# Second mixer of a two-block transformer kernel: the two value units of the differential heads side by side as a pair of 512 columns, the other heads' query and key units behind them, and the forget gate's logarithm later

## What is computed

```python
proj = h @ w_in                      # 1024 -> 3*512 + 3*512 + 8
dq, dk, dv = ...                     # differential: 4 heads, each with two query/key maps of 64, values of 128
fq, fk, fv = ...                     # forget gate: 8 heads of 64
f_logit = proj[..., o:o + FOX_HEADS].astype(jnp.float32) + b_f
cum = jnp.cumsum(jax.nn.log_sigmoid(f_logit), axis=1)
...
sd = jnp.einsum('bqhd,bkhd->bhqk', qd, dk) * (DIFF_HEAD_DIM ** -0.5) + bias
pd = jax.nn.softmax(jnp.where(causal, sd, NEG_2), axis=-1)
ad = pd[:, :, 0] - lam * pd[:, :, 1]
od = jnp.einsum('bhqk,bkhe->bqhe', ad, dv)
...
sf = jnp.einsum('bqhd,bkhd->bhqk', qf, fk) * (FOX_HEAD_DIM ** -0.5) + cq - cum_k
pf = jax.nn.softmax(jnp.where(causal, sf, NEG_2), axis=-1)
of = jnp.einsum('bhqk,bkhd->bqhd', pf, fv)
```

## Time and profile before

| | us |
|---|---|
| median of 3 runs | 845.45 (845.39 to 845.58) |
| the profiled execution | 845.1 |
| its span | 843.3 |
| TensorE busy | 829.5 (98%) |
| VectorE busy | 597.8 (71%) |
| ScalarE busy | 473.9 (56%) |
| mean granted clock of TensorE | 0.999 of full |

### The profile page before, as it was taken

One profiled execution on the slowest core, in us unless ns is written; L12 is line 12 of the kernel. 1 busy time (PEld: TensorE's weight loads), 2 busy tenths in 40 slices (PEclk: granted clock), 3 DMA queues, 4 the chain that ended last, 5 costly groups with the idle time before them and its releaser, 6 DMA issues.

```text
span 843.3 us, 13751 instructions
## 1 busy us (share of the span) xinstructions
PE 829.5 (98%) x5302; PEld 731.0 (87%) x5302; DVE 597.8 (71%) x797; ACT 473.9 (56%) x691; POOL 47.6 (6%) x50
## 2 busy tenths in 40 slices
PE   8999999999999999999999999999999999999997
PEld 7999998778777887999999998889888888888885
DVE  5548988758766576798677768777664786666664
ACT  5457874368765344766455546665675654444442
POOL 0025910000000000000000000000000000000000
PEclk9999999999999999999999999999999999999999
DMA  8734453335334446365545556244334355555431
GB/s 337 268 140 150 152 206 136 126 133 170 124 144 174 150 169 238 119 237 198 195 157 199 185 200 213 83 169 150 134 115 177 125 200 200 200 199 197 180 121 51
DMA packets 22596, 143.78 MB, mean 171 GB/s; under 512 B 2976, under 2 KB 3236, under 8 KB 6288
## 3 DMA queue, kind: packets, MB, share of 16 engines
q1 hardware_dynamic: 19872, 136.68, 45.5%
q0 software_dynamic: 1808, 4.73, 1.6%
q10 hardware_dynamic: 864, 1.64, 0.6%
HBM read 141.98 MB, written 1.84 MB: 171 GB/s over the span
## 4 chain that ended last, share of the span: by engine, by line
PE 92%; ACT 3%; DVE 2%; issue 1%; DMA 1%; ACTq 0%; DVEq 0%
PE pj L485 15%; PE pj L488 9%; PE pj L487 9%; PE pa L1006 7%; PE pa L1007 7%; PE pa L1008 7%; PE pj L490 6%; PE pj L489 6%; PE pj L1228 5%; PE pa L547 3%; PE pj L1230 2%; PE po L1228 2%; PE pj L612 2%; PE pj L614 1%; PE pj L618 1%
## 5 line engine op out<-in xcount | busy, mean ns | idle before, releaser
L1841 DVE TENSOR_TENSOR w_lo<-w_raw,w_hi 128x2048 fp32r<-128x2048 f32 x126 | 286.9, 2288 | 51.5 <-ACT w_hi L1274 51.1
L1274 ACT ACTIVATE w_hi<-w_raw 128x2048 fp32r<-128x2048 f32 x126 | 240.3, 1910 | 66.3 <-PE pa L1008 21.8
L485 PE MATMUL pj<-a_hl,w_hi 128*128 128x256 f32 x656 | 187.1, 285 | 0.0
L488 PE MATMUL pj<-a_hl,w_lo 128*128 128x256 f32 x656 | 185.9, 283 | 0.0
L487 PE MATMUL pj<-a_hl,w_hi 128*128 128x256 f32 x656 | 185.9, 283 | 0.0
L485 PEld LDWEIGHTS pj<-a_hl,w_hi 128*128 128x128 f32 x656 | 126.0, 192 | 1.4 <-issue 1.0
L487 PEld LDWEIGHTS pj<-a_hl,w_hi 128*128 128x128 f32 x656 | 126.0, 192 | 0.4
L488 PEld LDWEIGHTS pj<-a_hl,w_lo 128*128 128x128 f32 x656 | 126.0, 192 | 0.0
L1006 PE MATMUL pa<-w_hi,a_hl 128*128 128x512 f32 x280 | 109.6, 391 | 0.0
L1007 PE MATMUL pa<-w_lo,a_hl 128*128 128x512 f32 x280 | 109.3, 391 | 0.0
L1008 PE MATMUL pa<-w_hi,a_hl 128*128 128x512 f32 x280 | 109.1, 390 | 0.0
(11 more groups left out here) (288 smaller groups left out, 1165.1 us busy)
## 6 DMA issues: line engine op xcount, KB each, us to landing
w_raw<-stream SPq DMA_DIRECT2D x126, 1024.0 KB, 4.8
area<-gains POOLq DMA_DIRECT2D x4, 512.0 KB, 4.0
cst<-consts SPq DMA_DIRECT2D x1, 1117.0 KB, 10.2
area<-cmpw POOLq DMA_DIRECT2D x1, 1024.0 KB, 5.4
out<-x_tok SPq DMA_DIRECT2D x4, 256.0 KB, 2.0
t_wide<-t_rows POOLq DMA_DIRECT2D x1, 768.0 KB, 17.7
prm<-params SPq DMA_DIRECT2D x1, 574.5 KB, 7.9
x_tok<-x_in ACTq DMA_DIRECT2D x2, 256.0 KB, 5.5
```

The source lines that it names most:

```text
L485: pe.matmul(out_, a[0], a[1], start=first, stop=False)
L488: return pe.matmul(out_, wl, ah, start=False, stop=last)
L1274: act.activation(w_hi[:, slot, :], w_raw[:, slot, :], ACT.Copy).then_inc(S("w_hi_done"), 1)
L1841: dve.tensor_tensor(w_lo[:, slot, :], w_raw[:, slot, :], w_hi[:, slot, :].bitcast(F32), ALU.subtract)\
```

## The change

It does five things.

1. The order of units becomes dq0, dk0, dv0, dv1, dq1, dk1, then as before. By it the banks change: the pair dv takes `pj2` and `pj0`, dq1 takes `pj1`, dk1 `pj2`.
2. The units dv0 and dv1 hold 512 columns of half the input channels each and go through `wide_half`; ScalarE copies them with one `token_pair` after dv1. The second half of dv0 waits for the copy of dq0, and the first `d_apply` for both banks of the pair.
3. On TensorE dv1 stands where dq1 stood, dq1 behind the transposes of head 0, dk1 behind the apply of head 0, and fq0 behind the scores of head 2. The transposes of head 1 go ahead of the scores of head 2, those of head 2 ahead of `f_sums`.
4. On ScalarE Abs, Exp and Ln move from before the copy of head 0's transpose to behind `d_out(0)`, and both calls of `ahead` for dq1 and dk1 stand behind the exponentials of head 1.
5. On VectorE a call of `ahead` comes before the probabilities of head 0, the copy of dq1 behind the maxima of head 1, and the rows `lf8` behind the probabilities of head 2.

```diff
--- before.py
+++ after.py
@@ -42,7 +42,7 @@
          + [("wo", i) for i in range(4)])
 U_FFN1 = len(UNITS)
 U_FFN1_END = U_FFN1 + UP1 + DOWN1
-UNITS2 = ([(n, i) for i in range(2) for n in ("dq", "dk", "dv")]
+UNITS2 = ([("dq", 0), ("dk", 0), ("dv", 0), ("dv", 1), ("dq", 1), ("dk", 1)]
           + [(n, i) for i in range(2) for n in ("fq", "fk")] + [("fv", i) for i in range(2)] + [("wo2", i) for i in range(4)])
 U_FFN2 = U_FFN1_END + len(UNITS2)
 N_UNITS = U_FFN2 + UP2 + DOWN2
@@ -531,14 +531,14 @@
                           {} if i % 2 else dict(enumerate(pair)))
 
             def run_unit(name, gate=None):
-                if name[0] in ("sbv", "z"):
+                if name[0] in ("sbv", "z", "dv"):
                     wide_half(*name)
                     return
                 u = UIDX[name]
                 b, n = BANK[name]
                 unit_ready(u)
                 bank_free(b, n)
-                if name[0] in ("vv", "dv", "fv"):
+                if name[0] in ("vv", "fv"):
                     unit_a(u % SLOTS, b)
                 else:
                     unit_b(u % SLOTS, b, 8 if name[0] == "wo2" else 0, gate)
@@ -1098,8 +1098,9 @@
                 if h % 2 == 0:
                     claim(pe, "O", f"d{h // 2}")
                 await_read(pe, "T", f"d{h}")
-                if h % 2 == 0:
-                    await_value(pe, ("dv", h // 2))
+                if h == 0:
+                    await_value(pe, ("dv", 0))
+                    await_value(pe, ("dv", 1))
                 mm = weigh(po[:, (h % 2) * T:(h % 2 + 1) * T], dv[:, 0, h * P:(h + 1) * P],
                            dv[:, 1, h * P:(h + 1) * P], ptr2[h % 2][:, 0, :])
                 if h % 2 == 1:
@@ -1156,20 +1157,20 @@
             claim(pe, "O", "flog")
             pe.wait_ge(S("ws_ready"), 2)
             narrow_products(8)
-            run_unit(("dq", 1))
+            run_unit(("dv", 1))
             narrow_turn("flog_tok", 8)
             d_scores(1)
             d_turn(0)
+            run_unit(("dq", 1))
+            d_apply(0)
             run_unit(("dk", 1))
-            d_apply(0)
+            d_turn(1)
             d_scores(2)
-            d_turn(1)
-            run_unit(("dv", 1))
+            run_unit(("fq", 0))
             d_apply(1)
             d_scores(3)
-            run_unit(("fq", 0))
+            d_turn(2)
             f_sums()
-            d_turn(2)
             run_unit(("fk", 0))
             d_apply(2)
             d_turn(3)
@@ -1716,7 +1717,6 @@
             act.wait_ge(S("lam_sums"), 1)
             act.activation(lamv[:, 2:4], lamv[:, 0:2], ACT.Exp).then_inc(S("lam_exp"), 1)
             ahead(("dv", 0))
-            token_major(("dv", 0), dv[:, :, 0:256])
 
             def d_out(p):
                 await_psum(act, "O", f"d{p}")
@@ -1735,23 +1735,22 @@
                 act.activation(a_hi[:, 12 + j, :], fo(j), ACT.Copy).then_inc(S("mix2_hi"), 1)
 
             exps(8, sm2, pr2)
-            ahead(("dq", 1))
+            token_pair("dv", 0, dv)
             await_psum(act, "O", "flog_tok")
             read(act.activation(fl, po[:, 0:128].rearrange("p (b x) -> p b x", b=2)[:, :, 0:8], ACT.Copy), "O")
+            d_turned(0)
+            exps(9, sm2, pr2)
+            ahead(("dq", 1))
+            ahead(("dk", 1))
+            d_turned(1)
+            exps(10, sm2, pr2)
+            d_out(0)
             act.wait_ge(S("flx_ready"), 1)
             A.did(act.activation(lf_e, fl, ACT.Abs))
             A.sync()
             A.did(act.activation(lf_e, lf_e, ACT.Exp, scale=-1.0))
             A.sync()
             act.activation(lf_e, lf_e, ACT.Ln, bias=1.0).then_inc(S("lfe_ready"), 1)
-            d_turned(0)
-            exps(9, sm2, pr2)
-            ahead(("dk", 1))
-            ahead(("dv", 1))
-            d_turned(1)
-            exps(10, sm2, pr2)
-            token_major(("dv", 1), dv[:, :, 256:512])
-            d_out(0)
             ahead(("fq", 0))
             exps(11, sm2, pr2)
             await_psum(act, "O", "fcum")
@@ -2518,23 +2517,23 @@
             ahead(("dv", 0))
             d_soft(0)
             narrow_out("flog", 8)
+            ahead(("dv", 1))
             d_probs(0)
-            ahead(("dq", 1))
-            channel_major(("dq", 1), dq[:, 2:4, :], 64.0 ** -0.5)
             await_read(dve, "O", "flog_tok")
             tt(fl, fl, prm_("b_f").unsqueeze(1).to_broadcast([P, 2, 8]), ALU.add).then_inc(S("flx_ready"), 1)
             d_soft(1)
+            ahead(("dq", 1))
+            channel_major(("dq", 1), dq[:, 2:4, :], 64.0 ** -0.5, split_next=False)
+            d_probs(1)
+            channel_major(("dk", 1), dk[:, 2:4, :], split_next=False)
+            ahead(("dk", 1))
+            d_soft(2)
+            d_probs(2)
             dve.wait_ge(S("lfe_ready"), 1)
             for tb in range(2):
                 stt(lf8[:, tb], fl[:, tb].unsqueeze(1).to_broadcast([P, 16, 8]), 0.0,
                     lf_e[:, tb].unsqueeze(1).to_broadcast([P, 16, 8]), ALU.min, ALU.subtract)\
                     .then_inc(S("lf_ready"), 1)
-            d_probs(1)
-            channel_major(("dk", 1), dk[:, 2:4, :], split_next=False)
-            ahead(("dk", 1))
-            d_soft(2)
-            ahead(("dv", 1))
-            d_probs(2)
             d_soft(3)
             ahead(("fq", 0))
             channel_major(("fq", 0), fq[:, 0:2, :], 64.0 ** -0.5)
@@ -2660,6 +2659,8 @@
             return down(v["w_out"][0], i)
         if kind == "wo2":
             return down(v["w_out_2"][0], i)
+        if kind == "dv":
+            return rows4(w2[:, 1024:1536], i)
         return cols(w2, 512 * ("dq", "dk", "dv", "fq", "fk", "fv").index(kind) + 256 * i)
 
     def up1(j):
```

## The result

The changed kernel is slower: 851.78 us median of five runs (851.09 to 856.63) against 845.39 (845.28 to 845.58), a ratio of 1.0089 with a 95% interval of 1.0066 to 1.0111. The ratio is that of the mean times, 852.91 on 845.42; that of the medians is 1.0076. The runs themselves say something: those of before lie within 0.3 us, those of the change spread over 5.5 us, with mean granted clocks of 0.997, 0.997, 0.995, 0.995 and 0.991 from the fastest to the slowest.

What follows compares the result with a forecast made beforehand. TensorE was taken as the bound, busy 98% of 843.3 us. Terms +2.0 + 0.7 + 2.1 + 2.0 - 1.5 - 0.6 = +4.7 on 845.1 gave 849.8, with 0.35 for the median 850.1 us; range 847.4 to 852.2.

Steps and rivals of the forecast that it cites:

- The sign: Whole kernel: the change makes it slower, 94%, against faster 3% and same 3%.
- the waits: TensorE in the second mixer: head 0 transposes 2.0 us, head 2 scores 0.7, forget gate sums 2.1, first forget scores 2.0.
- The wide units: Two value units on TensorE: 24 matmuls of 512 columns instead of 48 of 256 gain 0.6 us together.
- the first wait: Transposes of head 0 on TensorE wait 2.0 us for VectorE's probabilities, now behind a low half.
- The sum for the queues: Whole kernel: waits added, the old 1.5 us wait and 0.6 us unit gain subtracted, +4.7 us, giving 849.8 us.
- the clock falls: Rival: TensorE at 1.2 GHz over the unit behind one wait, costing 5.84 us more, 856 us; 5%.
- the fourth wait: First forget scores on TensorE wait 2.0 us for VectorE's key copy, late through the chain behind the Ln.
- The third wait: Forget gate sums on TensorE wait 2.1 us for log-sigmoid rows, since ScalarE first reads heads 0 and 1 from PSUM.
- a switch at double the price: Rival: a ScalarE table switch costs 2.6 us, each late chain grows by 1.3, 852.7 us; 5%.
- The chains fit: Rival: ScalarE and VectorE deliver 2 us earlier, the old 1.5 us wait goes, faster at 843.35 us; 3%.
- only the early waits: Rival: the chain behind the logarithm has more cover, leaving +0.6 us, 846.05 us; 3%.

Runs made afterwards that it cites:

- change_narrow_2: Changed kernel with value units as 48 matmuls of 256 columns and ScalarE's second key unit high half ahead of its first value bank copy; 851.42 us, ratio 1.0083.
- log_early: Changed kernel with ScalarE's Abs, Exp and Ln back ahead of the copy of head 0's transpose; 851.81 us, ratio to before 1.0072.
- probs_log: Changed kernel with head 0's probabilities ahead of the low half on VectorE and the logarithm early on ScalarE; 847.25 us, ratio to before 1.0014.
- copy_first: Changed kernel with VectorE copying the first forget key unit out of its bank ahead of the low half; 850.02 us, ratio to before 1.0045.
- probs_first: Changed kernel with VectorE making head 0's probabilities ahead of the low half again; 848.19 us, ratio to before 1.0036.
- change_narrow: Changed kernel with the value units as 48 matmuls of 256 columns, a value bank copy ahead of ScalarE's high half; 852.23 us, ratio 1.0073.
- before_low_first: Kernel before the change, with only VectorE's low half moved ahead of the probabilities of head 0; 847.00 us, ratio 1.0026.
- three_undone: Changed kernel with head 0's probabilities ahead of the low half, the logarithm early and the key copy ahead of its low half; 843.62 us, ratio 0.9979.
- log_early_filled: log_early with dummy matmuls, 4 ahead of the transposes of head 0 and 3 ahead of the first forget scores; 847.67 us, ratio to before 1.0022.
- fill_waits: Changed kernel with 4 dummy matmuls ahead of each of head 0's transposes, the forget gate sums and the first forget scores; 850.42 us, ratio 1.0058.
- three_apply: three_undone with TensorE doing the apply of head 0 behind the second key unit; 843.42 us, ratio to before 0.9979.

## Why the prediction was right and wrong

**The sign, the places and the sizes of the waits were right.** All four are there: 1.97 (forecast 2.0), 0.55 (0.7), 1.85 (2.1), and 0.82 in the profiled execution or 2.32 where the clock did not fall (2.0). The wide units gained 0.55 us (0.6) and the first wait took that. The sum for the queues was 849.8 us; change_narrow_2, with its transposes at the same place and a full clock, took 849.74.

**The step that failed is the clock.** I set "the clock falls" beside the forecast as a rival of 5%, at the price of a whole unit, and wrote that the profile would show the clock at full. The argument against it was one wait, of 1.52 us, that had left it full. But the forecast itself put three waits of 2 us there. Those are longer than the only evidence, and the fall belonged in the sum, where it stood at nothing. In the profiled execution it measured 1.2 us, 0.98 in dq1 and 0.2 in the transposes before it; the other 1.48, in the key unit, were taken from the fourth wait. Against the 849.8 us of the sum this execution took 2.0 more; the later arrival at the mixer is 0.6 of that.

In the other runs the clock's part can only be estimated: a mean clock of 0.991 over 854.8 us is at most 7.7 us lost in the slowest run, 0.997 over 849.3 at most 2.5 in the fastest (at most, since the clock is low for a part of the waits too), and the 5.2 between them is nearly the 5.5 by which they differ. It is not the whole of each difference, for two runs with 0.995 are 1.8 us apart.

Dummies in the waits took the median to 850.42, and 4.1 us off log_early. The median of 851.78 lies inside the range of 847.4 to 852.2. The mean of the runs, 852.9, lies outside, and one run at 856.63 is where I had put the rival. That the median still lies inside is in part luck: without the fourth wait to take them up, the 1.5 us of the second fall would have put it at 853.3 (an estimate).

**The fourth wait had the right size, but only part of its cause.** I walked it from the Ln through the table load and head 3's exponentials. In the changed kernel the low half does wait 0.57 us for the high half at the end of that chain:

```profile
593.20 1.91 ACT L1275 ACTIVATE w_hi<-w_raw 128x2048 fp32r<-128x2048 f32 x1
```

```profile
595.14 2.29 DVE L1840 TENSOR_TENSOR w_lo<-w_raw,w_hi 128x2048 fp32r<-128x2048 f32 x1 [0.57 <-ACT w_hi L1275]
597.35 0.68 DVE L1853 TENSOR_TENSOR area<-pj,rbc 128x512 f32<-128x512 f32 x1
```

But I took the logarithm for the whole of it. probs_log and log_early have the logarithm early and the wait at 1.7 to 1.8 us all the same, against 2.3 in change_narrow_2, so its chain is worth 0.6. The rest is VectorE's own order: the low half stands in front of the copy. In log_early it follows the probabilities without a pause, and the copy follows it, though the key unit had ended at 593.07:

```profile
592.79 2.29 DVE L1840 TENSOR_TENSOR w_lo<-w_raw,w_hi 128x2048 fp32r<-128x2048 f32 x1
595.00 0.68 DVE L1853 TENSOR_TENSOR area<-pj,rbc 128x512 f32<-128x512 f32 x1
```

copy_first leaves the logarithm late; its copy started at 595.81, 0.2 us behind the key unit, and the wait is gone. The low half stood in front of the copy before the change too, but there it was done 1.1 us before the copy could start (587.19 + 2.29 against 590.62). Now it is late because the change moved the scores of head 3, and all behind them, behind a unit. That last step is read from the order of the queues; no run moves the scores alone.

**The third wait** was as forecast, from the apply of head 1 through `d_out(0)`, the Ln and the rows. The load of the table took 1.28 us, and the Ln began 1.29 us after the load had begun:

```profile
586.17 1.28 ACT L1753 ACT_TABLE_LOAD   x1
587.46 0.22 ACT L1753 ACTIVATE tiny<-tiny 128x16 f32<-128x16 f32 x1
```

So the rival of a switch at double the price is out. The figure of 2.66 us with a drain, from the Trainium skill, "ScalarE: Activation LUTs", "What ACT_TABLE_LOAD costs", is not what this trace has; the measurement decides.

**The other rivals.** "The chains fit" and "only the early waits" are out: the waits that are left in probs_first, with the fall of the clock behind one of them, cost 2.6 us over before. The order of the queues is the whole of the loss, by the waits themselves and by the clock that falls with them: with three edits of order the same change is at 843.62, below the kernel before.

What stays open is what decides in a given execution whether the clock falls behind a wait of about 2 us. No run changes that alone.

## What to carry to other kernels

When a unit of work is moved in one engine's queue, list for each hand-over what now stands ahead of the instruction that TensorE waits for: here a 2.3 us half of a weight unit in front of probabilities, and another in front of a copy, stood behind waits of 2.0 and 2.3 us, where the reshaped units give back 0.6. A wait of TensorE that comes near 2 us is to be priced at its length and a fall of the clock with it (9 of 13 in these profiles), and the fall costs in full where no later wait absorbs it. If the wait can't be removed, a few matmuls of no use in it brought back part of the loss in both kernels tried (1.4 and 4.1 us of the median).

## What the runs showed of the hardware

In the profiles of the changed kernel and the experiments, TensorE had 13 unfilled waits of 1.7 to 2.3 us in the mixer. The granted clock fell to 1.2 GHz at the end of nine of them or right behind (the changed kernel's 1.97 and 1.85; 1.98 and 1.73 in log_early; 1.98 in copy_first; 1.85 in probs_first; 1.8 in probs_log; 2.12 and 1.84 in change_narrow) and not behind four (1.85 in copy_first; 1.85 and 2.32 in change_narrow_2; 1.7 in before_low_first). Read in stretches of 1 us, the fall came between 0.6 us before the end of the wait and 1.3 us after it. Behind three waits of 1.39 to 1.52 us it did not fall, nor behind the five waits that were filled. One fall made the unit of 48 matmuls 0.98 to 2.1 us longer, and the transposes, sums or scores ahead of it by up to 0.9. The matmuls of 256 columns in a unit started 0.12 us apart at the full clock and 0.21 apart at the lower one (563.73 to 565.43 in the changed kernel).

A spread of the runs is a reading too. The runs lay 0.8 us apart in three_undone, 1.0 in log_early_filled and 1.5 in fill_waits; with open waits of 1.7 us and more 1.9 in change_narrow, 2.3 in probs_first, 2.8 in copy_first, 3.8 in probs_log, 3.9 in change_narrow_2, 4.1 in before_low_first and 5.5 in the changed kernel. It is no sharp sign: log_early with two open waits lay within 1.3, and there the mean clock was low in every run. three_apply with no open wait lay within 2.5, its slowest run at a mean clock of 0.996; and in the rounds of the experiments the kernel before had single runs of 847.0 to 847.5 us at 0.997, beside a median near 845.5, and its longest wait in the mixer is 1.5 us. These means suggest that the clock can fall without a wait near 2 us, though rarely; no profile shows where it fell in those runs.
